# A two-block transformer kernel: four score banks and head-by-head weight copies in local attention, separate buffers for the second modulation

## What is computed

```python
q, k, v = ...           # 16 query heads of 64, 4 key/value heads, axial rotary on q and k
# per block of 128 queries: 256 context keys and the window's latent keys
logits = [sink_logit] + [q . k_ctx / 8] + [where(|qpos - kpos| <= 128, q . k / 8, -inf)]
pr = softmax(logits)    # the sink takes its share but has no value
out = pr @ v            # over context and window keys
```

## Time and profile before

| | |
|---|---|
| median of 3 runs | 3156.13 us (3151.3 to 3163.28) |
| the profiled execution | 3155.31 us |
| its span in the trace | 3153.9 us |
| TensorE matmul busy | 2535.0 us (80%) |
| VectorE, ScalarE, GpSimd busy | 1238.2, 880.7, 106.9 us |
| DMA | 820.03 MB, mean 260 GB/s |
| mean granted TensorE clock | 0.922 of 2.4 GHz |

### The profile page before, as it was taken

How to read it: one execution, slowest core, us unless ns; L and a number is a source line. 1 busy time by engine, 2 the same in 40 slices (tenths; PEclk the granted TensorE clock), 3 DMA queues, 4 the chain that set the end, 5 groups by cost and what they waited for, 6 DMA issues and landing times.

```text
span 3153.9 us, 27811 instructions
## 1 busy us (share of the span) xinstructions
PE 2535.0 (80%) x11133; PEld 1463.4 (46%) x11133; DVE 1238.2 (39%) x2062; ACT 880.7 (28%) x1352; POOL 106.9 (3%) x175
## 2 busy tenths in 40 slices
PE   5988596869999996978587777769788997777786
PEld 4744474658888884544222222234474443222222
DVE  2376737469999996244200000032472012000001
ACT  3322323358878875132100000032031002000000
POOL 1011110010000001000100000000000000000000
PEclk8999798879999998988799989979889998999998
DMA  9399460169999995400699999842102433999997
GB/s 343 128 353 386 142 238 27 55 241 393 395 393 387 397 383 188 166 27 27 241 397 404 399 399 403 357 171 80 40 1 85 160 132 136 409 409 409 409 409 283
DMA packets 246923, 820.03 MB, mean 260 GB/s; under 512 B 11075, under 2 KB 11241, under 8 KB 246528
## 3 DMA queue, kind: packets, MB, share of 16 engines
q1 hardware_dynamic: 226688, 753.88, 62.0%
q0 software_dynamic: 14512, 46.28, 4.2%
q10 hardware_dynamic: 5584, 17.98, 1.5%
HBM read 780.20 MB, written 37.90 MB: 259 GB/s over the span
## 4 chain that ended last, share of the span: by engine, by line
PE 59%; DMA 24%; DVE 10%; ACT 3%; issue 2%; SPq 1%; POOL 0%; DVEq 0%; PEldq 0%; ACTq 0%; POOLq 0%
PE PS L245 56%; DMA ring<-in_moe_w_up 9%; DMA ring<-in_w_e_down 6%; DMA ring<-in_w_e_up 3%; DMA ring<-in_moe_w_gate 2%; DMA ring<-in_w_e_gate 2%; PE PS L1744 1%; DMA ring<-in_moe_w_down 1%; SPq L374 1%; DMA ring<-in_ada_w 1%; PE PS L550 1%; PE PS L2295 1%; DVE hgrn L935 0%; DVE SM L2349 0%; DVE SM L1353 0%
## 5 line engine op out<-in xcount | busy, mean ns | idle before, releaser
L410 DVE TENSOR_TENSOR cut<-ring,cut 128x1024 fp32r<-128x1024 f32 x424 | 501.5, 1220 | 181.9 <-ACT cut L402 170.8
L402 ACT CAST cut<-ring 128x1024 fp32r<-128x1024 f32 x424 | 438.3, 1054 | 266.3 <-PE PS L245 240.1
L245 PE MATMUL PS<-cut,xeT 128*128 128x512 f32 x1536 | 366.2, 395 | 3.2 <-DVE cut L410 3.2
L245 PEld LDWEIGHTS PS<-cut,xeT 128*128 128x128 f32 x1536 | 286.9, 189 | 68.1 <-DVE cut L410 6.3
L245 PE MATMUL PS<-ring,hidT 128*64 128x512 f32 (+1 forms) x1024 | 244.2, 628 | 72.2 <-DMA ring<-in_w_e_down 38.5
L245 PE MATMUL PS<-ring,xeT 128*64 128x512 f32 x1024 | 237.4, 609 | 74.5 <-DMA ring<-in_moe_w_up 41.0
L245 PE MATMUL PS<-ring,XE 128*32 128x512 f32 x1008 | 228.8, 604 | 67.4 <-DMA ring<-in_w_e_up 44.5
L245 PE MATMUL PS<-HT,ring 128*128 128x512 f32 (+2 forms) x576 | 206.4, 526 | 1.2 <-DVE HT L523 1.2
L245 PEld LDWEIGHTS PS<-ring,xeT 128*64 128x64 f32 x1024 | 75.8, 140 | 234.9 <-issue 172.6
L245 PE MATMUL PS<-cut,hidT 128*128 128x512 f32 x768 | 178.5, 392 | 4.5 <-DVE hidT L1753 4.5
L245 PEld LDWEIGHTS PS<-ring,hidT 128*64 128x64 f32 (+1 forms) x1024 | 72.5, 129 | 230.6 <-issue 177.0
(11 more groups left out here) (532 smaller groups left out, 2597.5 us busy)
## 6 DMA issues: line engine op xcount, KB each, us to landing
ring<-in_moe_w_gate SPq DMA_DIRECT2D x64, 2048.0 KB, 12.2
ring<-in_moe_w_up SPq DMA_DIRECT2D x64, 2048.0 KB, 11.9
ring<-in_moe_w_down SPq DMA_DIRECT2D x64, 2048.0 KB, 11.9
ring<-in_w_e_up SPq DMA_DIRECT2D x32, 2048.0 KB, 18.5
ring<-in_w_e_down SPq DMA_DIRECT2D x32, 2048.0 KB, 20.4
ring<-in_w_e_gate SPq DMA_DIRECT2D x31, 2048.0 KB, 18.4
ring<-in_ada_w SPq DMA_DIRECT2D x24, 2048.0 KB, 12.9
ring<-in_w_in SPq DMA_DIRECT2D x13, 2048.0 KB, 7.7
```

The costliest lines, as they stand in the source:

```text
L245: return pe.matmul(o, l, r, start=start, stop=stop, **kw)
L402: act.copy(self.bufs[i % len(self.bufs)][0], w).then_inc(self.high.sem, 1)
L410: dve.tensor_tensor(low, w, high.bitcast(F32), ALU.subtract).then_inc(self.low.sem, 1)
```

## The change

In local attention there are now four score banks (`u % 4`, banks 0 to 3), so the scores of pair p wait for both exponentials of pair p - 2. The transposed weights are laid out by head: head i of a pair goes into bank 4 + i with its four key blocks side by side, and each head is copied as soon as it is turned (`aT` is one tile of 2048 columns per group). Of a group's four copies ScalarE still makes three and VectorE one, but they are spread over the two steps. The transposes of a head now wait for the copy of the head two before (`taken(u - 2)`). The values alternate between banks 6 and 7, wait for all four copies at their beginning, and for the copy of the values two groups before. The strides of the value matmuls' moving operand change with the layout; counts and sizes of all instructions stay.

In the front, modulation unit 1 gets a place of its own and a load semaphore of its own (`mod_in_second`), so that GpSimd issues its memset and loads without waiting for `mod_done(0)`; `project_a_gpsimd` stands behind it on the same engine and has no wait of its own. `c_rows` moves to another address.

```diff
@@ -580,7 +580,7 @@
...
-    mod_place = {u: room("mod_place", 1536, 9984 if u < 2 else 12032) for u in (0, 2)}
+    mod_place = {u: room("mod_place", 1536, (9984, 14336, 12032)[u]) for u in range(3)}
     MODS = []
...
@@ -591,32 +591,33 @@
...
     mod_loads = [0]
-    for m in MODS:
-        mod_loads.append(mod_loads[-1] + 1 + 2 * len(m[3]))
+    for u, m in enumerate(MODS):
+        mod_loads.append(mod_loads[-1] + (1 + 2 * len(m[3]) if u != 1 else 0))
     mod_set = S.new("mod_ones", "pool")
-    mod_in = S.new("mod_in", "pool_q", 16)
+    mod_in, mod_in_second = S.new("mod_in", "pool_q", 16), S.new("mod_in_second", "pool_q", 16)
     mod_taken, mod_done = S.new("mod_taken", "dve"), S.new("mod_done", "dve")
...
     def mod_tiles(u):
-        place = mod_place[0 if u < 2 else 2]
+        place = mod_place[min(u, 2)]
         return place[:, 0:512], place[0:12, 512:1024], place[0:6, 1024:1536]
...
     def mod_gpsimd(u):
...
         sl = slice(512 * h, 512 * h + 512)
-        if u:
+        loaded = mod_in_second if u == 1 else mod_in
+        if u > 1:
             pool.wait_ge(*mod_done(u - 1))
...
         pool.wait_ge(*mod_set(u))
-        pool.dma_start(br, bias.rearrange("(a b) -> a b", b=D)[:, sl]).then_inc(mod_in.sem, 16)
+        pool.dma_start(br, bias.rearrange("(a b) -> a b", b=D)[:, sl]).then_inc(loaded.sem, 16)
         for row, g in gains:
             for r in range(2):
-                pool.dma_start(GB[row + r:row + r + 1, :], to_row(g)[:, sl]).then_inc(mod_in.sem, 16)
+                pool.dma_start(GB[row + r:row + r + 1, :], to_row(g)[:, sl]).then_inc(loaded.sem, 16)
     def mod_tensor(u):
...
@@ -633,7 +634,7 @@
...
         pe.wait_ge(*mod_taken(u))
-        pe.wait_ge(*mod_in(mod_loads[u + 1] - 1))
+        pe.wait_ge(*(mod_in_second(4) if u == 1 else mod_in(mod_loads[u + 1] - 1)))
         if u:
...
@@ -678,7 +679,7 @@
...
     c_in, consts_in, x_in = (S.new(n, "sp_q", 16) for n in ("c_in", "consts_in", "x_in"))
-    c_rows = room("c_rows", P, 11520, parts=32)
+    c_rows = room("c_rows", P, 13568, parts=32)
     ones_set, c_set = S.new("ones_set", "dve"), S.new("c_set", "dve")
...
@@ -2184,7 +2185,7 @@
...
     Sx = [room("weights", 512, 12288 + 512 * i) for i in range(4)]
-    aT = [[room("weights_T", 512, 14336 + 2048 * i + 512 * j) for j in range(4)] for i in range(2)]
+    aT = [room("weights_T", 2048, 14336 + 2048 * i) for i in range(2)]
     rope_t = room("rope", 256, 18944)
...
@@ -2270,41 +2271,47 @@
...
     even_taken, odd_taken, y_taken = S.new("even_taken", "dve"), S.new("odd_taken", "act"), S.new("y_taken", "act")
-    value_bank = bank(7)[:, 0:256]
     def pair_of(p):
...
         return p // 8, p % 8 * 2, p // 2, (2 * p, 2 * p + 1)
+
+    def taken(u):
+        return odd_taken(3 * (u // 4) + u % 4) if u % 4 < 3 else even_taken(u // 4)
+
+    def value_bank(g):
+        return bank(6 + g % 2)[:, 0:256]
     def window_tensor():
         def scores(p):
             qi, h, g, us = pair_of(p)
-            if p:
-                pe.wait_ge(*exped(2 * p - 2))
+            if p > 1:
+                pe.wait_ge(*exped(2 * p - 3))
             for i, u in enumerate(us):
                 pr = slice(64 * i, 64 * i + 64)
-                mm(bank(u % 3), QC[pr, h // 2, qi * P:(qi + 1) * P], KK[pr, h // 4, :], True, True).then_inc(scored.sem, 1)
+                mm(bank(u % 4), QC[pr, h // 2, qi * P:(qi + 1) * P], KK[pr, h // 4, :], True, True).then_inc(scored.sem, 1)
         def turn(p):
...
                 pe.wait_ge(*shared(u))
+                if u > 1:
+                    pe.wait_ge(*taken(u - 2))
                 for j in range(4):
-                    if g and (h + i) % 4 == 0:
-                        pe.wait_ge(*(odd_taken(3 * g - 3 + j) if j < 3 else even_taken(g - 1)))
-                    last = pe.transpose(bank(3 + j)[:, (h + i) % 4 * P:((h + i) % 4 + 1) * P], Sx[u % 4][:, j * P:(j + 1) * P], ident)
+                    last = pe.transpose(bank(4 + i)[:, j * P:(j + 1) * P], Sx[u % 4][:, j * P:(j + 1) * P], ident)
                 last.then_inc(turned.sem, 1)
...
         def values(p):
...
             if p % 2:
-                if g:
-                    pe.wait_ge(*y_taken(g - 1))
+                pe.wait_ge(*odd_taken(3 * g + 2))
+                pe.wait_ge(*even_taken(g))
+                if g > 1:
+                    pe.wait_ge(*y_taken(g - 2))
                 for j in range(4):
-                    pe.wait_ge(*(odd_taken(3 * g + j) if j < 3 else even_taken(g)))
                     for odd in range(2):
-                        last = mm(value_bank[64 * odd:64 * odd + 64, :], VC[:, j, 64 * (h // 4):64 * (h // 4) + 64],
-                                  aT[g % 2][j].rearrange("p (a b q) -> p a b q", a=2, b=2)[:, :, odd, :], j == 0, j == 3)
+                        last = mm(value_bank(g)[64 * odd:64 * odd + 64, :], VC[:, j, 64 * (h // 4):64 * (h // 4) + 64],
+                                  aT[g % 2].rearrange("p (a b j q) -> p j a b q", a=2, b=2, j=4)[:, j, :, odd, :], j == 0, j == 3)
                 last.then_inc(valued.sem, 1)
...
@@ -2317,23 +2324,23 @@
...
                     act.wait_ge(*turned(u - 4))
-                act.activation(Sx[u % 4], bank(u % 3), ACT.Exp, bias=st[:, i:i + 1], accum_out=st[:, 2 + i:3 + i])
+                act.activation(Sx[u % 4], bank(u % 4), ACT.Exp, bias=st[:, i:i + 1], accum_out=st[:, 2 + i:3 + i])
                 act.activation(st[:, 4 + i:5 + i], sink[:, h + i:h + i + 1], ACT.Exp, bias=st[:, i:i + 1]).then_inc(exped.sem, 1)
...
         def take(p):
             qi, h, g, us = pair_of(p)
-            if p % 2:
-                act.wait_ge(*turned(us[1]))
-                if g > 1:
-                    act.wait_ge(*valued(g - 2))
-                for j in range(3):
-                    act.copy(aT[g % 2][j], bank(3 + j)).then_inc(odd_taken.sem, 1)
+            for i, u in enumerate(us):
+                if u % 4 < 3:
+                    act.wait_ge(*turned(u))
+                    if u % 4 == 0 and g > 1:
+                        act.wait_ge(*valued(g - 2))
+                    act.copy(aT[g % 2][:, u % 4 * 512:u % 4 * 512 + 512], bank(4 + i)).then_inc(odd_taken.sem, 1)
         def keep(p):
...
                 act.wait_ge(*valued(g))
-                act.copy(YT1[:, h // 2 - 1:h // 2 + 1, qi * P:(qi + 1) * P], two(value_bank)).then_inc(y_taken.sem, 1)
+                act.copy(YT1[:, h // 2 - 1:h // 2 + 1, qi * P:(qi + 1) * P], two(value_bank(g))).then_inc(y_taken.sem, 1)
...
@@ -2343,10 +2350,10 @@
...
                 dve.wait_ge(*scored(u))
-                far = bank(u % 3)[:, (1 - qi) * P:(2 - qi) * P]
+                far = bank(u % 4)[:, (1 - qi) * P:(2 - qi) * P]
                 dve.tensor_tensor(far, far, swa[:, qi, (1 - qi) * P:(2 - qi) * P], ALU.add).then_inc(masked.sem, 1)
                 dve.wait_ge(*masked(u))
-                vs.add(dve.tensor_reduce(st[:, i:i + 1], bank(u % 3), AX.X, ALU.max))
+                vs.add(dve.tensor_reduce(st[:, i:i + 1], bank(u % 4), AX.X, ALU.max))
             dve.wait_ge(*vs.now)
...
@@ -2366,7 +2373,7 @@
...
                     dve.wait_ge(*valued(g - 2))
-                dve.tensor_copy(aT[g % 2][3], bank(6)).then_inc(even_taken.sem, 1)
+                dve.tensor_copy(aT[g % 2][:, 1536:2048], bank(5)).then_inc(even_taken.sem, 1)
...
         dve.wait_ge(*sink_in(0))
```

## The result

Seven runs of the changed kernel have a median of 3142.73 us (3137.26 to 3149.88) against 3156.13 before; the ratio is 0.9958, interval 0.9944 to 0.9971. In a later comparison it was 0.9946 (0.993 to 0.9962). The forecast was 3145. So 13 us came off (16.8 in the later comparison), but two terms of the sum were wrong in opposite directions, and the runs take them apart.

A forecast was written before the change was run, and what follows sets the result against it. The kernel was taken as a chain of stages, local attention bound by a ring of waits with no engine full. Attention 10.3 plus front 0.9 gave 11.2 off 3155.3, 3144.1; the median lies 0.8 above, so 3145 us; range 3130 to 3156.

The forecast's parts named there:

- Ramp: Local attention, from scores(0) to scores(4): 15 us (14 to 16.6) instead of 21.6, worth 6.6.
- Tail: Local attention, from scores(15) to its end: 14.6 us instead of 16.4, worth 1.8 (0 to 3.1).
- Steady part: Local attention, scores(4) to scores(15): 5.5 double steps of 11.2 us, 61.6 against 63.5, worth 1.9.
- I charge the same 2.3 us less 0.1: Local attention: the clock's cost per double step stays 2.3 us less 0.1, so 11.2 instead of 9.0 at 2.4 GHz.
- Where the idle falls: Local attention: TensorE's idle falls in one piece of about 2.4 us, in front of an even pair's transposes.
- Rival B: TensorE holds 2.4 GHz in local attention's steady part: attention 76.8 us, worth 24.7, kernel 3130.5; chance 17%.
- The second value bank: Local attention: values in two banks take away a wait for one 0.37 us copy, worth nothing.
- Front: Modulation front: a 3.3 us wait goes, `levels` ahead of the fourth ada piece costs 2.4, small loads nothing; gain 0.9.
- Rival C: The front gives its full 3.3 us, as `levels` is served behind the fourth ada piece: 3142.6 us; chance 10%.
- Carried whole: Local attention's saving of 10.3 us is kept whole: the expert stage behind it starts earlier by that much.
- D: TensorE stays at 1.2 GHz throughout local attention: double step 12.5 us, attention 103.9, kernel 3157.6; chance 6%.
- E: No gain arrives, as the stages behind are held by something that does not move: 3156 us; chance 7%.

The follow-up runs named there:

- e4_old_score_wait: Full change, but scores of a pair again wait for the first exponential of the pair before; 0.9965 of the kernel before, attention 94.5 us.
- The fill runs: Full change with `levels` and both small loads behind, plus two, four or six extra TensorE matmuls after even pairs' scores; attention 79.0, 80.9, 81.4 us.
- v1_one_value_bank: Full change, but all values in bank 7, waiting for the copy of the group before; attention 86.0 us, kernel 3139.93 us.
- e3_levels_behind: Full change, but `levels` and the two small loads wait for the copy of unit 1's sums; median 3132.42 us, 0.9919 of the kernel before.
- c3_all_mended: Full change with only `levels` issued behind the copy of unit 1's sums, and extra matmuls in steady idle pieces and behind pair 1's scores; 3130.84 us, 0.9918.

## Why the prediction was right, and where it was not

- **Ramp.** Predicted 15 us to scores(4), worth 6.6; measured 14.8, worth 6.8. Right, and e4_old_score_wait shows that the four banks' wait makes it.
- **Tail.** Predicted 14.6, worth 1.8; measured 14.5, worth 1.9.
- **Steady part.** Predicted 61.6 us, worth 1.9; measured 56.8, worth 6.7. This term was mis-sized, in two places. "The steady part at one clock is thus worth almost nothing (9.1 to 9.0)": a double step of the old order is 9.54 at one clock and one of the new 8.86, and over the stretch it is 52.7 against 49.7 us, 3.0. I had priced eight transposes at 1.09 where they stand between waits for copies; the row at 1426.87 with its 2.43 us was put down to the clock alone. And "I charge the same 2.3 us less 0.1" for the clock: over the same stretch it costs 63.5 - 52.7 = 10.8 us before and 56.8 - 49.7 = 7.1 after, 3.7 less. A part of that is the first double step, which kept 2.4 GHz.
- **Where the idle falls** was right: in front of the transposes of an even pair, waiting for L2337 (L2330 before), once a double step, and from the second on the clock falls there. Rival B, the clock up, did not come by itself. The fill runs show that its price was real: 49.7 us for the stretch against its 5.5 x 9.0 = 49.5.
- **The second value bank** was nothing, as said.
- **Front.** Predicted +0.9, measured -1.8 at MOD, and in the profiled executions nothing of it at the start of attention. The mechanism, `levels` in front of the fourth piece, was right and at 2.3 us rightly sized (2.4 predicted). The failed step is "Two small loads beside it (12 and 64 KB) are nothing": they cost 1.55 us. Their price was not that of their bytes: 0.06 MB at 0.40 MB per us would be 0.15. Some 0.3 us more of the piece's delay no run explains. The other omission is TensorE's level behind a late piece: the matmuls took 1.4 us more in the profiled execution. That is no fixed price: in v1_one_value_bank the piece came at 37.86 and they took 1.97, at 2.4 GHz.
- **The Trainium skill's rule** in "DMA: Bandwidth & Descriptors", on issuing engines, held: here `levels` on GpSimd's queue put off a piece on SyncE's by 2.3 us. Rival C, by which `levels` is served behind the fourth piece, fell.
- **Carried whole.** For attention it was, as far as the stage behind it: the output projection began at 1473.44 before and at 1457.73 after, 15.7 us earlier, and the front's 5 us of e3_levels_behind arrived too. The front's loss of 1.8 did not. Rivals D and E fell.

That 15.4 - 1.8 = 13.6 lies next to the 13.4 between the medians is chance: the loss did not reach attention, the profiled executions differ by 17.5, and the later comparison gave 16.8. The forecast of 11.2 was near in part by luck: the steady part was 4.8 too low and the front 2.7 too high.

## What to carry to other kernels

A buffer of its own lets not one instruction move but the whole queue behind it: here the gain of 3.3 us was eaten by three loads, the largest of them first read at 156 us, and one added wait turned a loss of 1.8 at MOD into a gain of 3.4, without touching a buffer. Where TensorE's clock falls behind an idle piece in a ring, the work behind it pays as well; two extra matmuls in that piece took 7 us off the stage, three in the wrong place added 9.7. And when a ring is priced at one clock, take the durations between waits from the rows where they wait, not from the row where they happen to run freely.

## What the runs showed of the hardware

- A load of 64 KB, one row of 512 bytes spread to 128 partitions, with one of 12 KB beside it, put off a piece on another queue by 1.55 us, while the 896 KB of `levels` put it off by 2.3. In the 2 us in which the rate was lowest (c3_all_mended, 12 to 14 us) the DMA share was 1.02 and the rate 156 GB/s, against 387 in the same 2 us of e3_levels_behind.
- The same four summing matmuls of the front took 1.98 us with the full change, 2.54 before it and 3.69 in c3_all_mended: the lengths of 2.4 GHz, a mix, and 1.2 GHz. 1.7 us lie between the extremes, on the path of the front, and the first and the last of these had the same 0.8 us of idle ahead of them.
- In local attention a TensorE with 1.57 us idle in each double step of 8.86 kept a granted clock of 1.00; with 2.77 idle in 10.24 it had 0.85. The old order with its 2.41 us cut to 1.11 us kept it in three of five double steps and lost it in two, so the length of the idle piece alone does not decide.
